# Gated feed-forward windows: 512-column matmuls over high and low x, and sums made by adding DMAs from POOL

## The reference

```python
def rms_norm(x, gain):
    xf = x.astype(jnp.float32)
    inv = lax.rsqrt(jnp.mean(xf * xf, axis=-1, keepdims=True) + NORM_EPS)
    return (xf * inv).astype(x.dtype) * gain

def swiglu(h, w_gate, w_up, w_down):
    return (jax.nn.silu(h @ w_gate) * (h @ w_up)) @ w_down

for l in range(DEPTH):                                   # DEPTH = 2
    x = x + 0.5 * swiglu(rms_norm(x, ffn1_norm[l]), ffn1_wg[l], ffn1_wu[l], ffn1_wd[l])
    ...                                                  # attention and short convolution
    x = x + 0.5 * swiglu(rms_norm(x, ffn2_norm[l]), ffn2_wg[l], ffn2_wu[l], ffn2_wd[l])
```

## Time and profile before

| | us |
|---|---|
| median of 3 runs | 2504.89 (2504.79 to 2505.01) |
| the profiled execution, its whole time | 2504.7 |
| its span in the profile | 2502.9 |
| PE busy | 2488.7 (99%) |
| DVE busy | 1991.0 (80%) |
| ACT busy | 1244.7 (50%) |
| POOL busy | 305.5 (12%) |
| PE's granted clock over the span | 0.999 of full speed |

### The profile page before, as it was taken

How to read it: one execution, slowest core, us unless ns; L and a number is a source line. 1 busy time by engine, 2 the same in 40 slices (tenths; PEclk the granted TensorE clock), 3 DMA queues, 4 the chain that set the end, 5 groups by cost and what they waited for, 6 DMA issues and landing times.

```text
span 2502.9 us, 36450 instructions
## 1 busy us (share of the span) xinstructions
PE 2488.7 (99%) x14212; PEld 2186.1 (87%) x14212; DVE 1991.0 (80%) x2830; ACT 1244.7 (50%) x1975; POOL 305.5 (12%) x250
## 2 busy tenths in 40 slices
PE   9999999999999999999999999999999999999998
PEld 7999988889999889999888899998888888888887
DVE  7878867778888688887777888876899786788873
ACT  6444444444444454444553544445577535654542
POOL 4000001320000000000023100000187221200002
PEclk9999999999999999999999999999999999999999
DMA  5333332223333323334323233334322333233331
GB/s 158 98 96 100 100 104 84 81 86 101 97 105 105 115 83 102 98 101 119 101 61 93 78 104 99 110 103 136 91 71 77 126 92 112 85 106 105 99 100 59
DMA packets 487297, 246.83 MB, mean 99 GB/s; under 512 B 42321, under 2 KB 483926, under 8 KB 486870
## 3 DMA queue, kind: packets, MB, share of 16 engines
q1 hardware_dynamic: 486674, 244.19, 33.9%
q10 hardware_dynamic: 452, 0.32, 0.0%
HBM read 240.27 MB, written 4.19 MB: 98 GB/s over the span
## 4 chain that ended last, share of the span: by engine, by line
PE 96%; DVE 2%; ACT 1%; DMA 0%; issue 0%; POOL 0%; DVEq 0%; ACTq 0%
PE bank L893 8%; PE bank L892 8%; PE bank L891 8%; PE bank L774 6%; PE bank L775 6%; PE bank L776 6%; PE psS L913 5%; PE psS L914 4%; PE psS L915 4%; PE bank L1454 3%; PE psT L957 2%; PE psT L959 2%; PE psT L958 2%; PE psT L774 2%; PE psT L775 2%; PE psT L776 2%
## 5 line engine op out<-in xcount | busy, mean ns | idle before, releaser
L2266 DVE TENSOR_TENSOR wlo<-raw,whi 128x1024 fp32r<-128x1024 f32 (+2 forms) x212 | 288.8, 1364 | 49.2 <-ACT whi L1581 46.0
L774 PE MATMUL bank<-xhl,whi 128*128 128x512 f32 x672 | 264.5, 394 | 0.0
L775 PE MATMUL bank<-xhl,whi 128*128 128x512 f32 x672 | 261.9, 390 | 0.0
L776 PE MATMUL bank<-xhl,wlo 128*128 128x512 f32 x672 | 261.8, 390 | 0.0
L891 PE MATMUL bank<-xshl,whi 128*128 128x256 f32 x840 | 237.8, 283 | 0.0
L892 PE MATMUL bank<-xshl,whi 128*128 128x256 f32 x840 | 237.7, 283 | 0.0
L893 PE MATMUL bank<-xshl,wlo 128*128 128x256 f32 x840 | 237.7, 283 | 0.0
L1581 ACT ACTIVATE whi<-raw 128x1024 fp32r<-128x1024 f32 (+2 forms) x209 | 214.4, 1029 | 37.3 <-PE bank L776 22.0
L2329 DVE TENSOR_TENSOR wlo<-tw,whi 128x1024 fp32r<-128x1024 f32 x140 | 171.6, 1226 | 62.5 <-ACT whi L1621 62.3
L913 PE MATMUL psS<-hhi,whi 128*128 128x512 f32 x488 | 191.7, 393 | 0.0
L914 PE MATMUL psS<-hlo,whi 128*128 128x512 f32 x488 | 191.6, 393 | 0.0
(11 more groups left out here) (703 smaller groups left out, 7184.7 us busy)
## 6 DMA issues: line engine op xcount, KB each, us to landing
raw<-in_ffn_wg SPq DMA_DIRECT2D x88, 512.0 KB
raw<-in_ffn_wu SPq DMA_DIRECT2D x88, 512.0 KB
raw<-in_w_in SPq DMA_DIRECT2D x53, 512.0 KB
raw<-in_w_mlp SPq DMA_DIRECT2D x40, 512.0 KB
raw<-in_ffn_wd SPq DMA_DIRECT2D x48, 256.0 KB
raw<-in_ffn_wd SPq DMA_DIRECT2D x24, 448.0 KB
raw<-in_ffn_wd SPq DMA_DIRECT2D x48, 192.0 KB
raw<-in_ffn_wd SPq DMA_DIRECT2D x48, 128.0 KB
```

The source lines that it names most:

```text
L774: pe.matmul(dest, a, rhs_hi(k), start=start and k == 0, stop=False)
L775: pe.matmul(dest, a, rhs_lo(k), start=False, stop=False)
L776: mm = pe.matmul(dest, b_, rhs_hi(k), start=False, stop=stop and k == tiles - 1)
L2266: dve.tensor_tensor(wlo[:, a:a + n], raw[:, a:a + n], whi[:, a:a + n].bitcast(F32), ALU.subtract).then_inc(s_split, 1)
```

## The change

In the fast windows of the four nets:

- `terms` issues two matmuls for a weight tile instead of three: hi weights by [hi x, lo x] as one of 512 columns into both halves of a bank, and lo weights by hi x, 256 columns, into the first half. Banks A, C and D are now 512 columns wide, and the result of a product is the sum of its two halves (a fold).
- The copies of A and the additions work on 512 columns. The first two additions write their halves to neighbouring tiles of `tmps` (`split1`), and a DMA from POOL with `accum_op` adds the one to the other (`k_fd`). The last fold of up is done by DVE, and the last gate quarter takes its second half through one more ACT copy (`part[1][:, 0:QT]`).
- The low parts of the side units: ACT writes the negated high part into `wlo`, and a DMA from POOL adds `raw` to it (`side_lo`, `k_sl`). DVE's `whole_lo` is gone. SP waits for `k_sl` before it loads a side unit again, and that slot's count in `s_split` comes with the weight sums.
- ACT's side copy `whole_hi(w, 1)` comes behind the copy of A, not ahead of it. Some semaphores are shared between stages to make room.

The core of the diff:

```diff
-                def terms(dest, wh, wl, at_w, moving, start, stop, resumed=False):
+                def terms(dest, wh, wl, at_w, moving, start, stop):
                     for k in range(4):
                         a, b_ = wh[:, at_w + k * P:at_w + (k + 1) * P], wl[:, at_w + k * P:at_w + (k + 1) * P]
-                        mh, ml = moving(k)
-                        pe.matmul(dest, a, mh, start=start and k == 0, stop=False, skip_group_check=resumed)
-                        pe.matmul(dest, a, ml, start=False, stop=False, skip_group_check=resumed)
-                        mm = pe.matmul(dest, b_, mh, start=False, stop=stop and k == 3, skip_group_check=resumed)
+                        mhl, mh = moving(k)
+                        pe.matmul(folds(dest), a, mhl, start=start and k == 0, stop=False, skip_group_check=True)
+                        mm = pe.matmul(dest[:, 0:QT], b_, mh, start=False, stop=stop and k == 3, skip_group_check=True)
                     return mm
...
                     act.activation(whi[:, a:a + n], raw[:, b_:b_ + n], ACT.Copy).then_inc(s_hi, 1)
+                    act.activation(wlo[:, a:a + n], raw[:, b_:b_ + n], ACT.Copy, scale=-1.0).then_inc(k_nh, 1)
...
-                    if w:
-                        whole_hi(w, 1)
                     act.wait_ge(k_pe, 5 * g + 1)
                     if g:
-                        act.wait_ge(k_ev, 4 * g - 3)
-                    act.activation(part[0][:, 0:QT], bank[0][:, 0:QT], ACT.Copy).then_inc(k_sn, 1)
+                        act.wait_ge(k_ev, 5 * g - 4)
+                    act.activation(part[0][:, :], bank[0][:, :], ACT.Copy).then_inc(k_sn, 1)
                     if w == 0:
                         hidden_hi(-1)
-                        whole_hi(0, 1)
+                    whole_hi(w, 1)
...
-                    act.activation(part[1][:, 0:QT], bank[0][:, 0:QT], ACT.Copy).then_inc(k_sn, 1)
+                    act.activation(part[1][:, :], bank[0][:, :], ACT.Copy).then_inc(k_sn, 1)
...
+                    act.wait_ge(s_used, q0 + c0 + u + 3)
+                    act.wait_ge(k_ev, 5 * g + 2)
+                    act.activation(part[1][:, 0:QT], bank[0][:, QT:S], ACT.Copy).then_inc(k_sn, 1)
...
-                    dve.tensor_tensor(tmp[1][:, t1], psT[:, 0:QT], part[0][:, 0:QT], ALU.add).then_inc(k_ev, 1)
-                    whole_lo(w, 1)
+                    dve.wait_ge(k_sn, 4 * g + 1)
+                    dve.tensor_tensor(split1(0, t1), folds(psT[:, 0:S]), folds(part[0][:, :]), ALU.add).then_inc(k_ev, 1)
...
-                    dve.tensor_tensor(tmp[3][:, t2], bank[1][:, 0:QT], part[1][:, 0:QT], ALU.add).then_inc(k_ev, 1)
+                    dve.tensor_tensor(split1(2, t2), folds(bank[1][:, :]), folds(part[1][:, :]), ALU.add).then_inc(k_ev, 1)
                     side_adds(w, 0)
...
-                    dve.tensor_tensor(tmp[1][:, t2], bank[0][:, 0:QT], inv[:, t2], ALU.mult).then_inc(k_ev, 1)
-                    dve.wait_ge(k_ev, 4 * g + 1)
-                    dve.tensor_tensor(tmp[1][:, t1], tmp[1][:, t1], inv[:, t1], ALU.mult).then_inc(s_gs, 1)
+                    dve.wait_ge(k_sn, 4 * g + 4)
+                    dve.tensor_tensor(tmp[0][:, t2], bank[0][:, 0:QT], part[1][:, t1], ALU.add).then_inc(k_ev, 1)
+                    dve.wait_ge(k_ev, 5 * g + 3)
+                    dve.wait_ge(k_fd[0], 16 * (g + 1))
+                    dve.tensor_tensor(tmp[0][:, :], tmp[0][:, :], inv[:, :], ALU.mult).then_inc(s_gs, 1)
...
-                    dve.tensor_tensor(tmp[3][:, t1], bank[1][:, 0:QT], part_f[0][:, :], ALU.add).then_inc(k_ev, 1)
-                    dve.wait_ge(k_ev, 4 * g + 4)
-                    dve.tensor_tensor(tmp[3][:, :], tmp[3][:, :], inv[:, :], ALU.mult).then_inc(s_us, 1)
+                    dve.tensor_tensor(part[2][:, :], bank[1][:, :], part[2][:, :], ALU.add).then_inc(k_ev, 1)
+                    dve.wait_ge(k_ev, 5 * g + 4)
+                    dve.tensor_tensor(tmp[2][:, t1], part[2][:, t1], part[2][:, t2], ALU.add).then_inc(k_ev, 1)
+                    dve.wait_ge(k_ev, 5 * g + 5)
+                    dve.wait_ge(k_fd[1], 16 * (g + 1))
+                    dve.tensor_tensor(tmp[2][:, :], tmp[2][:, :], inv[:, :], ALU.mult).then_inc(s_us, 1)
...
+            def side_lo(g, i, n):
+                a, b_ = (2 * i + 1) * UNIT, (2 + i) * UNIT
+                pool.wait_ge(k_nh, 2 * g + i + 1)
+                pool.dma_start(wlo[:, a:a + n], raw[:, b_:b_ + n], accum_op=ALU.add).then_inc(k_sl[i], 16)
+
+            def net_sums(nf):
+                net = NETS[nf]
+                side_lo(net.first_g, 0, net.side_cols(0, 0))
+                for w in range(net.fast):
+                    g = net.first_g + w
+                    pool.wait_ge(k_ev, 5 * g + 1)
+                    pool.dma_start(tmp[0][:, 0:QT], tmp[1][:, 0:QT], accum_op=ALU.add).then_inc(k_fd[0], 16)
+                    side_lo(g, 1, net.side_cols(w, 1))
+                    pool.wait_ge(k_ev, 5 * g + 2)
+                    pool.dma_start(tmp[2][:, QT:S], tmp[3][:, QT:S], accum_op=ALU.add).then_inc(k_fd[1], 16)
+                    if w + 1 < net.fast:
+                        side_lo(g + 1, 0, net.side_cols(w + 1, 0))
```

More of the change, by code:

```diff
@@ L178, in build @@
         rows3 = dist[:, P:2 * P]
-        tmp = [sb(f"tmp{i}", S) for i in range(4)]
-        hid13h = sb("hid13h", S, F32R, off=tmp[0].manual_sbuf_range[0])
-        hid13l = sb("hid13l", S, F32R, off=tmp[2].manual_sbuf_range[0])
+        tmps = sb("tmps", 4 * S)
+        tmp = [tmps[:, i * S:(i + 1) * S] for i in range(4)]
+        hid13h = sb("hid13h", S, F32R, off=tmps.manual_sbuf_range[0])
+        hid13l = sb("hid13l", S, F32R, off=tmps.manual_sbuf_range[0] + 2 * S * 4)
         aligned(ROW)
@@ L201, in build @@
         folds = lambda a: a.rearrange("p (h n) -> p h n", h=2)
+        part.append(sb("part2", S, off=first_inv.manual_sbuf_range[0]))
         assert cvec.manual_sbuf_range[0] >= identr.manual_sbuf_range[0] + 4 * S
@@ L455, in build @@
         k_lo = sem("fast_weights_lo_ready")
+        k_nh = sem("side_weights_hi_negated")
+        k_sl = [sem(f"side_weights_lo_landed{i}") for i in range(2)]
+        k_fd = [sem("gate_quarter_folded"), sem("up_quarter_folded")]
         k_pe = sem("fast_product_done")
@@ L596, in side_rows @@
                     slot_free(c, q0)
+                    if w:
+                        sp.wait_ge(k_sl[i], 16 * (net.first_g + w))
                     unit = SIDES[w][i]
@@ L616, in ffn @@
                 for m in range(KC):
+                    if m in (2, 3):
+                        sp.wait_ge(k_sl[m - 2], 16 * (net.first_g + FAST))
                     down_rows(LAST_AT + m, -1, m)
@@ L1684, in hidden_hi @@
                     act.wait_ge(s_h, fb + tile + 1)
-                    act.activation(chunk(hhi, tile % HT), tmp[3][:, :], ACT.Copy).then_inc(s_hh, 1)
+                    act.activation(chunk(hhi, tile % HT), tmp[3 if w < 0 else 2][:, :], ACT.Copy).then_inc(s_hh, 1)
                 def fast_window(w):
@@ L2261, in _, with split @@
         def _(dve):
-            def split(c, q, tiles=8):
+            def split(c, q, tiles=8, units=1):
                 dve.wait_ge(s_hi, q + c + 1)
```

177 lines of the change are left out of this document (83 added, 94 removed).

## The result

The changed kernel takes **2538.8 us** (median of 4 runs, 2537.3 to 2540.4); before, 2504.9. The ratio is 1.0135 (95% interval 1.0118 to 1.0153): slower, as forecast, and inside the stated range, but by 33.9 us where the forecast had 16.1. The profiled execution took 2540.4 us, 35.7 more than that of before.

What follows compares the result with a forecast made beforehand. The prediction took TensorE (PE) as the bound, busy 2488.7 of 2502.9 us with 96% of the last chain. It summed 2504.7 - 13.1 (joined matmuls) + 29.4 (hand-overs) = 2521.0 us, range 2497 to 2595.

Steps and rivals of the forecast that it cites:

- The gain: PE's matmuls in the nets' fast windows: 1960 joined pairs at 0.3533 us for triples at 0.360, 13.1 us saved.
- Hand-over A: Before the dwh product PE waits for DVE's 512-wide bank add: 0.32 us in 40 windows, 12.8 us lost.
- Hand-over B: Before the third product PE waits for ACT's copy of bank 0: 0.27 or 0.56 us, 20 windows each, 16.6 us.
- The rest: Extra DVE and ACT work, side and up weights' loads, semaphores: covered by idle time, nothing added to the forecast.
- The adding DMA: POOL's DMA for the up fold, wanted first: taken as 3.5 us of 3.9 available, so it fits; bounds 1.7 to 4.9.
- rival 1: Adding DMAs are late: at 5.0 us each they delay window ends, +58 us, 2579 us; chance 0.22.
- Rivals 2 and 3: 2: wider hand-overs absorbed, 2491.6 us, chance 0.14; 3: restart free, Hand-over B's chain 0.2 us shorter, 2501.4 us, chance 0.10.
- the restart: PE's slow first matmul after a wait: 0.17 us, taken from one wait in the profile before.
- Rival 4: POOL's building of DMAs slows DVE's 1024-column subtraction, window end 1.1 us later, 2579 us; chance 0.06.
- the cover of the up weights' load: Load issued 1.15 us later after dwl; DVE's 0.71 us idle time before L2329 takes up the lateness.
- The sum: 2504.7 us before, less 13.1 from joined matmuls, plus 29.4 lost at both hand-overs: 2521.0 us, chance 0.48.

Runs made afterwards that it cites:

- half of the load: Kernel without adding DMAs, with only half of each up weights' load in the fast windows (256 KB in place of 512): 2522.7 us, ratio 1.0072.
- dwl early: Changed kernel with DVE's last low part (dwl) moved behind the up fold's quarter add: 2549.8 us; the same without adding DMAs: 2543.8 us.
- both moves: Changed kernel with ACT's copy of bank 0 ahead of the hidden tile's high part and DVE's dwl behind the up fold's quarter add: 2521.4 us.
- bank copy first: Changed kernel with ACT's copy of bank 0 (L1695) ahead of the hidden tile's high part: 2538.8 us.

## Why the prediction was right and wrong

- **The gain, 13.1 us: right** as the intervals go; what reaches the end is 4.2 to 8.1. The formula for an isolated matmul in the Trainium skill (TensorE: Matmul & The Clock Gate, Back-to-back issue gap) would give a pair of 0.325 us as an estimate; the trace has 0.351.
- **Hand-over A, 0.32 us in a window of three first tiles: right by itself.** Window 1541.75 lost 0.33, and 14.0 to 15.0 us stand against 12.8 in three kernels whose up weights were on time (half of the load, *dwl early* with and without adding DMAs). In the changed kernel it was 21.3. It is 20.3 with *both moves* as well, where the loads were on time but PE no longer lost time at B.
- **Hand-over B, 16.6 us in 40 windows: right** with no adding DMAs (15.8); in the changed kernel 20.2, and 6.0 more behind windows of four or five last tiles, where the forecast had nothing lost.
- **The step that failed first is in "The rest"**: the up weights' load, 1.15 us later, "DVE's 0.71 us of idle time before L2329 takes up what comes late". It doesn't. The late load delays the sums (L2322 and L2325 after), ACT's high part waits for the second of them, and the 0.71 is idle time behind that. What was free was the gap from DVE's second sum to ACT's start; in the kernel before, same window as the earlier trace rows:

```profile
1597.30 0.69 DVE L2322 TENSOR_TENSOR tw<-tw,raw 128x512 f32<-128x512 f32 x1
```

It ends at 1597.99 and ACT's high part starts at 1598.35, held by the copy ahead: 0.36 us, not 0.71. The load's own time was too short as well. Its last bytes do move some 3.2 us after its issue (3.15 at the median before, 3.21 after, by its packets), but the first up sum gets to start later than that: 3.99 us after the issue in the 47 windows of the kernel after in which it waited, 4.02 in the 44 without any adding DMA (medians). The kernel before had almost no room for 1.15 us. The window behind the forecast's:

```profile
1606.37 0.39 SPq L581 DMA_DIRECT2D raw<-in_ffn_wu  x1
...
1610.26 1.23 DVE L2319 TENSOR_TENSOR tw<-raw 128x1024 f32<-128x1024 f32 x1
```

That is 3.89 us; at the median of the 66 windows that have one ahead it is 4.06, the forecast's own window had 4.56, and in eleven windows the sum already waited, by 0.04 to 0.26 us. And this load is released by dwl at the end of the same window, so lateness goes round. After, 47 loads made DVE wait, and 7.4 us came of it.
- **The adding DMA, 3.5 us of 3.9: the bound was right, the value wrong where it counted.** The median of both folds is 3.2 us, but the fold that is wanted first, the up fold, is issued beside the gate weights' load. A window of the kernel after, timelines of SP, POOL, DVE, ACT and PE:

```profile
1463.62 0.49 SPq L579 DMA_DIRECT2D raw<-in_ffn_wg  x1
...
1465.72 0.87 POOL L3348 DMA_DIRECT2D tmps<-tmps  x1 [4.84 <-DVE tmps L2433]
...
1470.49 0.69 DVE L2453 TENSOR_TENSOR tmps<-tmps,inv 128x512 f32<-128x512 f32 x1 [1.25 <-DMA tmps<-tmps]
...
1472.48 0.58 ACT L1695 ACTIVATE part<-bank 128x512 f32<-128x512 f32 x1
...
1473.21 0.47 PE L893 MATMUL bank<-xshl,whi 128*128 128x512 f32 x1 [1.22 <-ACT part L1695]
```

4.8 us after its issue, 1.25 too late, and PE waits 1.22. In 26 of 70 windows it was late. The 70 up folds land after 2.7 to 6.1 us, and sooner the longer the gate weights' load is under way: at the median 4.34 us where the fold is issued less than 1 us behind that load (late in 10 of 12 windows), 3.46 at 1 to 1.8 us (7 of 21), 2.73 at 1.8 to 2.5 us (5 of 29, the window shown among them). In the other 8 no such load is near and 4 were late; what delays those wasn't followed. That is rival 1 in a third of the windows: 11 us, where its price for all was 58. The forecast asked whether this DMA is late in all windows or in none. Its landing spreads, and a margin of 0.4 us doesn't cover the spread. The fit of the Trainium skill (2.3 us for 128 KB as an estimate; DMA: Bandwidth & Descriptors, Anatomy of one DMA) was further off than the rows' 3.5.
- **Rivals 2 and 3** (absorbed, restart free) fell: waits of 0.3 us stand at both places, and the restart costs 0.26 + 0.07 - 0.11 (the time DVE was late) = 0.22 us, more than the 0.17 taken.
- **Rival 4** fell: DVE's subtraction of 1024 columns L2314 runs beside one of POOL's DMA issues for more than half of its time in 66 windows and lasts 1.225 us there at the median.

So the direction and both hand-overs taken by themselves were right. The steps that failed are the cover of the up weights' load, put at nothing and worth 7.4 us, and the adding DMA, put at nothing ("it fits") and worth 11.1. The sum treated A, B and the load as terms that add. They are points of rings, as far as the runs tell: a term can vanish without gain (bank copy first) and two moves that gain nothing alone can gain 17 us together.

## What to carry to other kernels

Before pricing a longer step, follow what it releases round to itself, DMA loads included: if the way round (here 14.7 us) is as long as the bound engine's work in the period (14.0 to 14.7), each tenth of a microsecond on it can be paid in every turn, wherever the wait shows. Count a load's cover up to the start of the instruction that it frees (here 4.0 us from its issue), not up to its last bytes (3.2). When a step is moved, list both what it releases and what it now stands ahead of; four of these experiments missed for want of one of the two. A transfer that must land within 0.4 us of its mean time was late in 26 of 70 turns here, most often where it was issued close behind another transfer.

## Of the hardware, not expected

- With the two adding DMAs issued at 1465.72 and 1466.33 under way and the gate weights' load of 1463.62 about over, the DMA engines were fully taken at little over half the GB/s of a load. Stretches of 0.5 us of the kernel after (busy times, PEclk, DMA share, GB/s), then one of the kernel before during the gate weights' load:

```profile
1468.00:1468.50 0.50, 0.50 (x4) 0.41 (x3) 0.50 (x2) 0.24 (x1) 0.00 (x0) 1.00 1.03 185
1468.50:1469.00 0.50, 0.50 (x3) 0.39 (x3) 0.47 (x2) 0.00 (x0) 0.00 (x0) 1.00 1.08 190
```

```profile
1601.00:1601.50 0.50, 0.50 (x7) 0.50 (x6) 0.50 (x1) 0.00 (x0) 0.00 (x0) 1.00 1.12 340
```

- POOL is held 0.87 us by the issue of a fold's DMA and 1.19 us by that of a side row's; its busy time went from 305.5 to 551.5 us.
- A PE that waits shows less idle time than it loses, by some 0.23 us a wait, as its last matmul's end (0.28 after its start, where the next would follow at 0.12) and the slow first interval (0.31 for 0.24) count as busy.
